# Front stages of a hybrid decoder step rebuilt: sample columns in the u and states stages, one block for carry, y and z

## What is computed

```python
h = rms_norm(x, lw['norm_mix_g'])
proj = h @ lw['w_in']
q, k, v, u, g_att, g_s5 = jnp.split(proj, IN_SPLITS, axis=-1)
...
bu_re = jnp.einsum('blgc,gpc->blgp', ug, bb_re)
bu_im = jnp.einsum('blgc,gpc->blgp', ug, bb_im)
bu_re = bu_re.at[:, 0].add(lb_re * h0_re - lb_im * h0_im)
bu_im = bu_im.at[:, 0].add(lb_re * h0_im + lb_im * h0_re)
_, _, hr, hi = lax.associative_scan(combine, (ar, ai, bu_re, bu_im), axis=1)
y = (jnp.einsum('blgp,gcp->blgc', hr, c_re) - jnp.einsum('blgp,gcp->blgc', hi, c_im)
     + d_skip * ug)
...
z = jax.nn.gelu(s5y, approximate=False)
s5o = z * jax.nn.sigmoid(z @ lw['w_glu'] + lw['b_glu'])
```

## Time and profile before

| what | us |
|---|---|
| median of 3 runs | 5053.72 (5047.71 to 5055.49) |
| the profiled execution, its own time | 5064.18 |
| its span in the trace | 5062.4 |
| TensorE busy | 3650.2 (72%) |
| VectorE busy | 3119.5 (62%) |
| ScalarE busy | 1526.2 (30%) |
| norm, u, Toeplitz, states (from the span's start to) | 57.08, 244.84, 300.07, 471.30 |
| carry, store wait, y, z (to) | 493.44, 545.89, 719.21, 748.81 |
| the three chunks and PEER (to) | 5062.4 |

### The profile page before, as it was taken

How to read it: one execution, slowest core, us unless ns; L and a number is a source line. 1 busy time by engine, 2 the same in 40 slices (tenths; PEclk the granted TensorE clock), 3 DMA queues, 4 the chain that set the end, 5 groups by cost and what they waited for, 6 DMA issues and landing times. The chain is left out here.

```text
span 5062.4 us, 44057 instructions
## 1 busy us (share of the span) xinstructions
PE 3650.2 (72%) x13408; PEld 2059.8 (41%) x13408; DVE 3119.5 (62%) x6957; ACT 1526.2 (30%) x3824; POOL 1340.6 (26%) x1167
## 2 busy tenths in 40 slices
PE   6965689696766576686665875757777777777776
PEld 4543466574433343342444764424322222222221
DVE  4145210315777877677888657768766666666664
ACT  3111010312324432142444433221333333333333
POOL 0000000002222223223222323224444444444443
PEclk9955559898987788898887887879999999999999
DMA  2011314248866687888556999769999999999997
GB/s 80 35 19 1 3 51 150 80 162 307 353 246 221 241 354 275 343 346 340 198 206 240 399 372 387 316 251 368 408 419 417 416 410 415 412 411 407 408 411 314
DMA packets 281661, 1416.06 MB, mean 280 GB/s; under 512 B 44226, under 2 KB 85666, under 8 KB 144322
## 3 DMA queue, kind: packets, MB, share of 16 engines
q0 software_dynamic: 159344, 1129.94, 56.2%
q1 hardware_dynamic: 121698, 283.19, 16.5%
q10 hardware_dynamic: 384, 0.13, 0.0%
HBM read 1369.87 MB, written 40.93 MB: 279 GB/s over the span
## 5 line engine op out<-in xcount | busy, mean ns | idle before, releaser
L807 POOL DMA_INDIRECT arena<-in_uv,arena x1056 | 1272.1, 1205 | 2486.6 <-DVE arena L918 1591.5
L908 DVE CUSTOM_DVE_ANT_0 arena<-arena 128x1024 f32<-128x1024 f32 x1056 | 1288.3, 1221 | 499.8 <-DMA arena<-in_uv,arena 469.9
L1024 PE MATMUL ps<-arena 128*128 128x512 f32 (+1 forms) x2320 | 1108.6, 624 | 417.2 <-ACT arena L993 417.2
L1091 PE MATMUL ps<-arena 128*128 128x256 f32 (+2 forms) x3456 | 1125.3, 487 | 222.4 <-DMA arena<-in_w_stat 54.3
L1091 PEld LDWEIGHTS ps<-arena 128*128 128x128 f32 x3456 | 693.9, 204 | 618.5 <-issue 448.9
L1024 PEld LDWEIGHTS ps<-arena 128*128 128x128 f32 (+1 forms) x2320 | 423.3, 191 | 1101.9 <-ACT arena L993 638.6
L918 DVE SCALAR_TENSOR_TENSOR arena<-arena 128x1024 f32<-128x1024 f32 x476 | 608.6, 1279 | 35.8 <-ACT arena L983 35.8
L974 ACT ACTIVATE arena<-arena 128x2 f32<-128x2 f32 x528 | 107.2, 203 | 1723.6 <-DVE arena L908 1723.2
L983 ACT ACTIVATE arena<-arena 128x1 f32<-128x1 f32 x1056 | 253.4, 287 | 17.8 <-ACT arena L974 0.7
L813 POOL DMA_DIRECT2D arena<-in_iota x1 | 0.7, 704 | 933.0 <-POOLq L1972 933.0
L974 ACT ACT_TABLE_LOAD x157 | 201.4, 1283 | 4.7 <-issue 1.9
(11 more groups left out here) (251 smaller groups left out, 3758.6 us busy)
## 6 DMA issues: line engine op xcount, KB each, us to landing
arena<-in_w_stat SPq DMA_DIRECT2D x216, 512.0 KB, 7.3
arena<-in_cache_k SPq DMA_DIRECT2D x64, 512.0 KB, 11.0
arena<-in_cache_v SPq DMA_DIRECT2D x64, 512.0 KB, 12.0
arena<-in_w_mov SPq DMA_DIRECT2D x14, 2048.0 KB, 13.0
arena<-in_uv,arena POOLq DMA_INDIRECT x1056, 13.1
arena<-in_x SPq DMA_DIRECT2D x16, 512.0 KB, 4.6
arena<-scr_s POOLq DMA_DIRECT2D x64, 128.0 KB, 12.9
scr_s<-arena SPq DMA_DIRECT2D x16, 384.0 KB, 12.2
```

The lines of the kernel that those rows point to most:

```text
L807: pool.indirect_dma_start(ring[s % RING], None, dr["uv"], bass.IndirectOffsetOnAxis(ap=idx[:, g % 4, j:j + 1], axis=0)).then_inc(row_in[s ...
L908: nc.vector.tensor_tensor_reduce(ring[s % RING][:, 0:D], ring[s % RING][:, 0:D], h2r[:, b % 2, :], 1.0, 0.0, ALU.mult, ALU.add, act_in[:, ...
L1024: last = nc.tensor.matmul(ps[0:m, 4 * (b % 2) + c, :], diag[:, n % 4, 0:m], ring[s % RING][:, D + 512 * c:D + 512 * (c + 1)], start=start, ...
L1091: last = nc.tensor.matmul(ps[:, bank, 0:w], wbuf[m % NWB][:, kc * P:(kc + 1) * P], moving[:, kc, :], start=(kc == 0), stop=(kc == KC - 1))
```

## The change

All eight front stages but Toeplitz are rewritten, and the blocks of carry, y and z become one.

Norm: the nine row blocks have a buffer each and are all loaded at the start. ScalarE squares all nine, then the small steps are done for blocks 0 to 3 and 4 to 8 at a time; the even blocks are scaled by ScalarE, the odd ones by VectorE; the transposes use all eight banks. `subln` is loaded here. u: the sample step comes first in each half and takes all 32 rows at once; it goes to `us_st`, out to `scr_us` and back in 8-row form (four small DMAs), and is brought to partitions 64 to 127 of eight further columns of `ug` by 64 matmuls. States: the sample columns stand beside the chunk columns, so one matmul of 136 columns does both; the second pair of transposes, `st4` and its copy are gone.

```diff
-                    for s in range(ST8 + NNEW):
+                    for s in U_STEPS:
...
-                        rows = P if s < ST8 else NSEQ
+                        rows = P if s < ST8 else NS
...
+                pe.wait_ge(us_in, 16 * NNEW)
                 for g in range(G):
-                    last = nc.tensor.transpose(ps[0:64, 7, g * NSEQ:(g + 1) * NSEQ],
-                                               us_tok[0:NSEQ, g], ident[0:NSEQ, 0:NSEQ])
+                    last = nc.tensor.matmul(ps[64:P, 7, g * NSEQ:(g + 1) * NSEQ], us_tok[0:NSEQ, g].rearrange("q t c -> q (t c)"),
+                                            ident[0:NSEQ, 0:NSEQ], start=True, stop=True)
...
                     for par_ in range(2):
                         half = slice(64 * par_, 64 * par_ + 64)
                         for ri in range(2):
-                            nc.tensor.matmul(ps[half, 2 + gp % 2, ri * P:(ri + 1) * P], st[:, gp % 2, ri, half],
-                                             ug[:, 2 * gp + par_, :], start=True, stop=True)
-                            last = nc.tensor.matmul(ps[half, 2 + gp % 2, 256 + ri * NSEQ:256 + (ri + 1) * NSEQ],
-                                                    st4[0:64, gp % 2, ri, half], ua[0:64, 2 * gp + par_, :],
-                                                    start=True, stop=True)
+                            last = nc.tensor.matmul(ps[half, 2 + gp % 2, ri * NUG:(ri + 1) * NUG], st[:, gp % 2, ri, half],
+                                                    ug[:, 2 * gp + par_, :], start=True, stop=True)
```

```diff
             def _(sp):
                 sp.wait_ge(rec, N_CARRIED)
                 sp.dma_start(out["s5_prompt"], hh[:, :, :, NCH:NCH + 1], allow_slow_non_contiguous=True).then_inc(st_out, 16)
+                sp.wait_ge(rec, N_LATE + 8)
                 sp.dma_start(out["s5_sample"], hs.rearrange("p r g q -> p (r g q)")).then_inc(st_out, 16)
+                for c in range(KC):
+                    sp.wait_ge(z_free, z_no(c, 2))
+                    sp.dma_start(z_all[:, c, :], z_st[:, c % 2, :]).then_inc(z_out[c % 2], 16)
+                    if c == KC - 3:
+                        sp.wait_ge(y_ready, NYS + 2 * (G // 8))
+                        for m in range(NWB):
+                            load_tile(sp, m)
+                        load_hT(sp, 0)
                 sp.wait_ge(st_out, 32)
...
+                for k in range(2):
+                    sp.wait_ge(z_out[k], 16 * (KC // 2))
+                load_zT(sp, 0)
...
+                def turn_z(c):
+                    pe.wait_ge(y_free, NYS + 2 * c + 2)
+                    if c >= 2:
+                        pe.wait_ge(z_free, z_no(c - 2, 2))
+                    for b in range(2):
+                        bank = 4 + 2 * (c % 2) + b
+                        for s in range(4):
+                            last = nc.tensor.transpose(ps[:, bank, s * P:(s + 1) * P], z_tok[:, 4 * b + s, c * P:(c + 1) * P], ident[:, :])
+                        last.then_inc(z_ready, 1)
...
+                    if q >= 1:
+                        turn_z(q - 1)
+                    if q >= 2:
+                        turn_zs(q - 2)
+                turn_z(KC - 1)
+                turn_zs(KC - 2)
+                turn_zs(KC - 1)
```

More of the change, by code:

```diff
@@ new lines, in hybrid_step, with load_tile, stat_tile @@
+        n_fa, n_fv = 0, 0
+        def load_tile(sp, m):
+            if m < N_TILES:
+                if m >= NWB:
+                    sp.wait_ge(acc_ready, m - NWB + 1)
+                sp.dma_start(wbuf[m % NWB], dr["w_stat"][stream[m]]).then_inc(w_in[m % NWB], 16)
+        def stat_tile(pe, m, bank, moving, w):
+            pe.wait_ge(w_in[m % NWB], 16 * (m // NWB + 1))
+            for kc in range(KC):
+                last = nc.tensor.matmul(ps[:, bank, 0:w], wbuf[m % NWB][:, kc * P:(kc + 1) * P], moving[:, kc, :],
+                                        start=(kc == 0), stop=(kc == KC - 1))
+            last.then_inc(acc_ready, 1)
@@ L683, in hybrid_step @@
+                take_z(0)
+                for c in range(1, KC):
+                    take_z(c)
+                    take_zs(c - 1)
+                take_zs(KC - 1)
         scr_k = nc.dram_tensor("scr_k", (H, P, T), F32, kind="Internal").ap()
```

435 lines of the change are left out of this document (207 added, 228 removed).

## The result

The changed kernel took 4852.1 us (median of four: 4859.6, 4810.6, 4845.6, 4858.6) against 5054.4 for the one before: ratio 0.9586, 95% interval 0.9529 to 0.9642. Forecast were 4843 and a range of 4803 to 4873. The profiled execution took 4859.6 us with a span of 4857.8, so the two profiled executions lie 204.6 us apart, where the prediction's sum said 210.6. Term by term they don't agree that well.

A forecast was written before the change was run, and what follows sets the result against it. Eight front stretches run one after another, each bounded by the engine that ends it. Gains 21 + 38.6 + 83 + 68 = 210.6 us take the profiled 5064.2 to 4853.6, the median 5053.7 to 4843; range 4803 to 4873.

The forecast's parts named there:

- The frame: First 748.8 us: eight stretches one after the other, nothing hidden behind another; the rest keeps its length.
- Norm: Norm stage: all blocks loaded at once, then serial small steps and take-outs; 36.3 us for 57.1, gain 21.
- u: u stage: two sample steps for eight, small matmuls taken as 5 us; gain 38.6 us (34 to 41).
- States: States stage: full clock, VectorE's four scan batches set the end; 88 us for 171.2, gain 83 (55 to 85).
- rival (a): States stage stays at 1.2 GHz or is paced worse: 102 to 116 us, total 4857 to 4871; chance 14%.
- Carry to GLU: Carry, store, y and z up to the first GLU matmul: 209.2 us for 277.5, gain 68 (59 to 74).
- the sample y's term: Carry to GLU: 64 sample groups at 0.83 us, 53.3 us, with VectorE's carry hidden under them.
- the store ... is over long before SP needs the queue for z: Carry to GLU: the 45.5 us prompt state store starts at 18.4, ends well before 85; removes 52.5 us idle.
- Rival (d): Carry to GLU: 4-byte store slowed by other traffic delays zT's reload; at 390 us eats the whole gain; chance 1%.
- prompt y and turns: Carry to GLU: prompt y stays 120.0 us, z and sample z turns inside it add 14.4 (11 to 20).
- the tail: From the last y matmul to GLU: Gelu, turn, copy, SP's queue, zT's reload; 21.5 us (16 to 26) for 29.6.
- Rival (b): Prompt y gets the full clock from the transposes dropped into it: 49 us less, 4794; chance 11%.

The follow-up runs named there:

- the split kernel: Changed kernel with only the sample columns taken out of the states stage's wide matmul, as 8-column matmuls of their own, 128 rows high: 4876.6 us.
- the bursts: 24 transposes of the identity, result unread, added to the changed kernel ahead of the prompt y: 4810.6 us; ahead of the sample y instead: 4850.7 us.

## Why the prediction was right, and where it was not

**The frame** held: eight stretches one after the other, the sum made from their ends, nothing given back later.

**Norm** was 1.4 us shorter than forecast (34.9 for 36.3), since VectorE's scaling takes 0.7 us, near the lower of my two bounds, where I took 1.1. The loads, Squares and first roots ended at 19.2, as worked out, and that is luck: I had one Square behind the last load, but ScalarE worked on the nine of them with hardly a break from 4.4 to 17.5, which by chance ended when the last load did.

**u** was 6.9 us short, and one term carries it: the 128 small passes took 12.2 us, above even my upper bound of 10. I had taken the old transposes of the same data (0.035 each) as the near row. Their records have the same form as the new ones (weights of 8 rows and 64 columns, 8 columns streamed), at the same clock, so neither the form nor the clock is why they were the wrong row; what differs is that they are transposes, and that they write rows 0 to 63. Which of the two counts is not shown. The new passes took 0.059 us each at first, and from 179.8, when the clock fell under them, 0.107. The row that was near is the 0.31 us for two narrow passes, which I had as the bound, but halved for the full clock. In all eleven traces where these passes stand in one row the clock fell 2 to 5 us into them, and they took 9.5 to 12.2 us; this one is the longest.

**States**, the largest term, came out at 86.0 for 88.3, and what I named as the bound (VectorE's four batches, no wait between them) is in the trace. The clock rose in the changed kernel, 5.4 us in, as I had it. But the two cases were wrongly priced. I took 2.6 us for a pair at 1.2 GHz, with each pass at the price of the transposes of the earlier trace rows; the trace has such pairs, at 1.73 us, because the passes of the two column halves run beside each other: their records start two at a time, 0.01 us apart. At that price TensorE stays ahead of VectorE at either clock, and rival (a) is 90 us by the estimate above, not 102 to 116. So the forecast for this stage did not hang on the clock, and the chance of 14% was put on a price that the stage doesn't have. At 1.00 the pair was quicker too (0.99 for 1.3 us), which gained 2 us only, as VectorE is the bound.

My reason for the old stage's cost was only half right. I wrote that the narrow matmuls break the row of full ones. It was their height more than their presence: with narrow matmuls of full height the stage takes 91.5 us, or 103.9 in the split kernel, where the clock stayed at 0.50. That this is near rival (a)'s 102.5 is chance, for that kernel has narrow matmuls and (a) had none.

**Carry to GLU** was 14.5 short, and 13.7 of it is the sample y's term, 67.0 us for 53.3. The step "the store ... is over long before SP needs the queue for z" held in its words (it ran from 350.6 to 397.5, and the first z rows leave at 448.9), but it put the store at nothing. I looked at who waits for the store's end and not at who shares the DMA engines with it while it runs; the instruction fetch isn't in the program's text, but it is in the trace's DMA queues. Rival (d) had the right neighbour, the 4-byte store under the work of others, but the wrong victim. The rest held: prompt y and turns 133.7 for 134.4, the tail 23.3 for 21.5.

**Rival (b)** was given 11%. No trace has it, but one of eight executions of the changed kernel lay 48 us under the others' middle, where (b) would put it, and the bursts show that the prompt y, once it has the full clock, kept it for 40 to 76 us. The argument against (b), that the clock could not live with the half-height matmuls, was too simple: in the changed kernel they and the turns between them did not bring it up in 133.7 us, yet it stayed up over them for long. What ends it is open: it fell 50 us into the prompt y behind the burst of 24 transposes, and 40 us into it in the kernel without transposes in the sample y, both times with TensorE busy without a break.

**The median** was 9 us over the forecast. Six of it are the sums' (21.4 short in two terms, 3.4 over in two others, 11.9 from the rest of the program); the other three are that the forecast took 10.5 us off for a profiled execution's excess over its median, where the changed kernel's had 7.5.

## What to carry to other kernels

A transfer in 4-byte pieces is not free because nothing waits for its end: look in the trace for what shares the DMA engines, instruction fetches too, and copy such data to one contiguous tile first (here 7 to 13 us of the median for one VectorE copy), or issue the store where the engines fetch less often. A wait of TensorE ahead of a long stretch at half clock is a place for a few transposes that nobody reads, and in the kernels here the clock was held best with full-height parts spread evenly rather than in one piece. Before a clock case gets a chance and a price, ask whether the engine that ends the stage would notice it; in the states stage VectorE would have had 4 us of it. Between matmuls in a row, keep the height the same: a narrow matmul of 128 rows was cheaper than one of 64.

## What was not expected of the hardware

- An instruction fetch of 16 KB took 11.5 us beside the 4-byte store, for 1.0 without it, and TensorE stood still for 13.5 and 17.4 us in two traces of the same kernel, and for as little as 3.0 in others with the same store.
- Between two full-height matmuls a narrow one of 64 rows costs 0.27 us more at 0.50 than one of 128 rows with the same columns.
- The same prompt y stayed at 1.00 for 74 us in two executions and fell after 40 in a third; with 20 spread transposes more, five times lay within 12 us.
- Small passes with 8 rows and 64 weight columns take 0.059 us at full clock and 0.107 at half, for 0.035 of a transpose of the same form at full clock, and in eleven of eleven traces the clock fell under a row of 128 of them.
- Passes that write the two halves of the output rows ran two at a time (starts 0.01 us apart), so that at 0.50 a pair of groups took 1.73 us where 2.6 were expected.
